# Moving the preparation of the output projection's right operands into the retention

## The reference

```python
for layer in range(DEPTH):                      # DEPTH = 2, x is (1024, 1024) float32
    h = rms_norm(x, norm_g[layer])
    z = h @ w_in[layer]
    ...                                         # attention -> oa, ya
    qr, kr, vr = ...                            # 4 retention heads of 128
    orr = bidirectional_retention(qr, kr, vr, lg_f, lg_b)
    orr = head_group_norm(orr, ret_gn_w[layer])
    yb = (jax.nn.silu(gr) * orr) @ w_branch_ret[layer]
    gates = jax.nn.sigmoid(gm).reshape(b, s, N_BRANCHES, d)
    merged = gates[:, :, 0] * ya + gates[:, :, 1] * yb
    x = x + merged @ w_out[layer]
return rms_norm(x, final_norm_g)
```

## Time and profile before

| what | value |
|---|---|
| median of 3 runs | 1856.19 us (1851.78 to 1858.89) |
| the profiled execution | 1854.67 us |
| its span in the profile | 1852.8 us |
| mean granted TensorE clock | 0.989 |
| PE busy | 1755.4 us (95%) |
| PE weight loads busy | 1555.3 us (84%) |
| DVE busy | 1262.6 us (68%) |
| ACT busy | 800.3 us (43%) |
| POOL busy | 671.9 us (36%) |
| moved by DMA | 113.08 MB, mean 61 GB/s |

### The profile page before, as it was taken

The page is one execution under the profiler, slowest core; times in us unless marked ns, Lnnn a source line. Parts: engine busy times, 40 slices in busy tenths (PEclk is TensorE's granted clock), DMA queues, the critical chain, the costliest instruction groups (busy, mean ns, idle before and its releaser), DMA issues.

```text
span 1852.8 us, 30202 instructions
## 1 busy us (share of the span) xinstructions
PE 1755.4 (95%) x10592; PEld 1555.3 (84%) x10592; DVE 1262.6 (68%) x2626; ACT 800.3 (43%) x1791; POOL 671.9 (36%) x581
## 2 busy tenths in 40 slices
PE   6799999999999999999989998999999999999986
PEld 5688978899999888887787888889999998888865
DVE  7878578725544387769986877795345544867798
ACT  4378448722122243333344873684222123433333
POOL 0048217724233323223601771484224322232240
PEclk9999999999999999999999999999999999999998
DMA  7000000011011323224130001001011023222322
GB/s 269 23 13 12 27 23 24 24 47 47 23 34 35 131 66 100 80 90 160 46 118 24 24 1 50 12 12 47 24 46 45 23 92 114 67 82 86 131 80 91
DMA packets 136666, 113.08 MB, mean 61 GB/s; under 512 B 16481, under 2 KB 115041, under 8 KB 136545
## 3 DMA queue, kind: packets, MB, share of 16 engines
q1 hardware_dynamic: 134144, 106.20, 17.9%
q10 hardware_dynamic: 2400, 5.31, 0.8%
HBM read 90.52 MB, written 20.97 MB: 60 GB/s over the span
## 4 chain that ended last, share of the span: by engine, by line
PE 71%; DVE 17%; issue 4%; POOL 3%; ACT 3%; DMA 2%; POOLq 0%; SPq 0%; DVEq 0%; ACTq 0%
PE ps L758 17%; PE ps L760 17%; PE ps L759 16%; PE ps L894 4%; PE ps L883 4%; PE ps L907 2%; DVE xh L2163 2%; PE ps L909 2%; PE ps L1000 2%; POOL pp L612 1%; PE ps L984 1%; DVE hT_lo L2150 1%; DVE us L1895 1%; DVE pT_lo L1807 1%; DVE lsum L2141 1%
## 5 line engine op out<-in xcount | busy, mean ns | idle before, releaser
L758 PE MATMUL ps<-w_hi,hT_hi 128*128 128x256 f32 (+1 forms) x1280 | 390.9, 305 | 13.8 <-DVE hT_lo L1666 4.8
L760 PE MATMUL ps<-w_hi,hT_lo 128*128 128x256 f32 (+1 forms) x1280 | 376.6, 294 | 0.0
L759 PE MATMUL ps<-w_lo,hT_hi 128*128 128x256 f32 (+1 forms) x1280 | 376.3, 294 | 0.0
L758 PEld LDWEIGHTS ps<-w_hi,hT_hi 128*128 128x128 f32 x1280 | 244.8, 191 | 19.0 <-DVE hT_lo L1666 7.0
L759 PEld LDWEIGHTS ps<-w_lo,hT_hi 128*128 128x128 f32 x1280 | 245.1, 191 | 0.3
L760 PEld LDWEIGHTS ps<-w_hi,hT_lo 128*128 128x128 f32 x1280 | 244.5, 191 | 0.0
L612 POOL TENSOR_SCALAR pp<-pp,rrc 128x1024 f32<-128x1024 f32 x128 | 144.1, 1126 | 164.5 <-DVE rrc L1812 157.3
L1807 DVE TENSOR_TENSOR pT_lo<-ps,pT_hi 128x512 fp32r<-128x512 f32 x256 | 164.1, 682 | 26.5 <-ACT pT_hi L1307 25.2
L558 POOL TENSOR_SCALAR w_hi<-raw 128x1024 fp32r<-128x1024 f32 x65 | 69.2, 1064 | 290.5 <-PE ps L760 254.6
L1799 DVE TENSOR_REDUCE nmx<-ps 128x1 f32<-128x1024 f32 x128 | 154.0, 1203 | 2.6 <-PE ps L883 2.6
L894 PE MATMUL ps<-idf,pp 128*128 128x128 f32 x1024 | 140.6, 278 | 15.5 <-DVE pT_lo L1807 9.0
(11 more groups left out here) (215 smaller groups left out, 4103.5 us busy)
## 6 DMA issues: line engine op xcount, KB each, us to landing
raw<-w_in SPq DMA_DIRECT2D x167, 256.0 KB, 3.3
xs<-xh SPq DMA_DIRECT2D x2, 4096.0 KB, 16.9
ys<-y_st SPq DMA_DIRECT2D x32, 256.0 KB, 2.1
hb<-ys SPq DMA_DIRECT2D x16, 512.0 KB, 4.6
xh<-xs SPq DMA_DIRECT2D x8, 1024.0 KB, 7.0
raw<-w_a SPq DMA_DIRECT2D x16, 256.0 KB, 3.2
raw<-w_r SPq DMA_DIRECT2D x16, 256.0 KB, 3.3
w<-w_o SPq DMA_DIRECT2D x4, 1024.0 KB, 6.2
```

The source lines that it names most:

```text
L758: nc.tensor.matmul(outp, ah, bh, start=(start and i == 0), stop=False)
L759: nc.tensor.matmul(outp, ah, bl, start=False, stop=False)
L760: last = nc.tensor.matmul(outp, al, bh, start=False, stop=(stop and i == len(pairs) - 1))
```

## The change

The right operands are no longer made in the output projection. During the retention they are made one row piece at a time and written to a tensor `wos` in the chip's memory, and in the output projection they are loaded from there, as they are, into the places that PE reads.

There are 28 items per layer: 4 row pieces k of w_out (K_R = 4, piece k belongs to head k) times 7 products in the order R_ORDER. One item is 128 rows x 512 columns of high and of low part. For each item: POOL makes the sum where it has one (`right_sum`, items 2 to 6 of a piece), ACT the high part (`right_hi`), DVE the low part (`right_lo`), and ACT issues the write to memory (`right_put`, 512 KB). ACT also loads piece k of w_out (`right_load`, 1 MB). Two staging places alternate, so item n waits until item n - 2 has been written (`r_free`). R_FIRST, R_SECOND and R_NEXT say at which tile each item stands: all seven of piece 0 in head 0's first pass at tiles 2 to 8, items 0, 1, 2 of piece h + 1 in head h's second pass at tiles 3, 5, 7, and items 3, 4, 5, 6 of piece h in head h's first pass at tiles 1, 3, 5, 6. The hardware loops of POOL, ACT and DVE over the heads are written out. The two `keep_out` steps wait for the items and their writes of that head.

```diff
+K_R = 4
+R_ORDER = (1, 5, 0, 2, 3, 4, 6)
+N_R = K_R * N_P
+R_FIRST = {2: 0, 3: 1, 4: 2, 5: 3, 6: 4, 7: 5, 8: 6}
+R_SECOND = {3: 0, 5: 1, 7: 2}
+R_NEXT = {1: 3, 3: 4, 5: 5, 6: 6}
...
+        def r_free(eng, L, n):
+            if L * N_R + n >= 2:
+                eng.wait_ge(r_out[n % 2], 16 * ((L * N_R + n) // 2))
...
 @@ sync: output projection
+                def right_in(p, halves=(0, 1)):
+                    for h in halves:
+                        c = right_wide(p, h)
+                        for s, to in enumerate(right_slot(p, h)):
+                            src = wos[p, :, s, 1024 * h:1024 * h + 1024].rearrange("p (b c) -> p b c", c=c)
+                            sp.dma_start(to.bitcast(F32), src).then_inc(o_r[R_SLOT[p]][h], 16)
...
+                    if m == 2:
                         sp.wait_ge(e_lo, (L + 1) * 2 * N_S)
+                        for b in range(2):
+                            sp.wait_ge(r_out[b], 16 * (L + 1) * (N_R // 2))
+                        right_in(0, (0,))
...
+                sp.wait_ge(g_p, x7 + 3)
+                right_in(0, (1,))
                 x_block(0, 1)
                 sp.wait_ge(g_p, x7 + 4)
                 x_block(1, 1)
+                sp.wait_ge(g_p, x7 + 7)
+                right_in(1)
                 x_block(0, 0)
+                right_in(2)
                 sp.wait_ge(d_mg, (L + 1) * N_G)
                 x_block(1, 0)
+                for p in range(3, N_P):
+                    if p != 4:
+                        sp.wait_ge(o_done, L * (4 * N_P) + 4 * N_P + 4 * ({3: 0, 5: 1, 6: 2}[p] + 1))
+                    right_in(p)
...
 @@ gpsimd
+                def right_sum(k, i):
+                    n = k * N_P + i
+                    blocks = RIGHT[R_ORDER[i]]
+                    if len(blocks) == 1:
+                        return
+                    pool.wait_ge(r_in, 16 * (L * K_R + k + 1))
+                    r_free(pool, L, n)
+                    (r, c, q) = blocks
+                    a, b = (wo_raw[:, 2 * x[0] + x[1]] for x in (r, c))
+                    nc.gpsimd.tensor_tensor(r_total(n), a, b, ALU.add if q > 0 else ALU.subtract).then_inc(r_sum, 1)
...
                             else:
                                 fill_lo(i % 2, i, n0 + U_C + fills * N_C + N_C + i)
+                        at = R_FIRST if h == 0 else R_NEXT
+                        if t in at:
+                            right_sum(h, at[t])
...
-                with pool.Fori(0, RH - 1) as h:
+                for h in range(RH - 1):
                     fill_qk(h)
+                    for i in R_SECOND.values():
+                        right_sum(h + 1, i)
                     rotate(h + 1, h)
...
 @@ scalar
+                def right_hi(k, i):
+                    n = k * N_P + i
+                    if len(RIGHT[R_ORDER[i]]) == 1:
+                        act.wait_ge(r_in, 16 * (L * K_R + k + 1))
+                        r_free(act, L, n)
+                    else:
+                        act.wait_ge(r_sum, (L * K_R + k) * 5 + i - 1)
+                    nc.scalar.copy(r_rows(n)[0], r_src(n)).then_inc(r_hi, 1)
+                def right_put(k, i):
+                    n = k * N_P + i
+                    act.wait_ge(r_hi, L * N_R + n + 1)
+                    act.wait_ge(r_lo, L * N_R + n + 1)
+                    a = 2 * (n % 2)
+                    act.dma_start(wos[R_ORDER[i], :, :, 512 * k:512 * k + 512], quad(ur_lo, 4)[:, a:a + 2].bitcast(F32)).then_inc(r_out[n % 2], 16)
+                def right_steps(at, t, k):
+                    if t - 1 in at:
+                        right_put(k, at[t - 1])
+                    if t in at:
+                        right_hi(k, at[t])
...
+                        right_steps(R_FIRST if done is None else R_NEXT, t, h)
...
 @@ vector
+                def right_lo(k, i):
+                    n = k * N_P + i
+                    dve.wait_ge(r_hi, L * N_R + n + 1)
+                    hi, lo = r_rows(n)
+                    V.tensor_tensor(lo, r_src(n), hi.bitcast(F32), ALU.subtract).then_inc(r_lo, 1)
+
                 def keep_out(h, half):
+                    for b in range(2):
+                        dve.wait_ge(r_out[b], 16 * ((L * N_R + min(h + 2, K_R) * N_P + 1 - b) // 2))
...
+                        at = R_FIRST if done is None else R_NEXT
+                        if t in at:
+                            right_lo(h, at[t])
...
+                        if h + 1 < RH and t in R_SECOND:
+                            right_lo(h + 1, R_SECOND[t])
```

More of the change, by code:

```diff
@@ L168, in build @@
             pT_lo = sb(p2, "pT_lo", [2, T, 256], F32R)
+        with ExitStack() as pz:
+            sb(pz, "below_wo", [2 * SEQ])
+            wo_raw = sb(pz, "wo_raw", [4, 512])
         ur_hi = sb(ctx, "ur_hi", [KA, SEQ], F32R)
@@ L205, in build @@
             w12 = sb(pg, "w12", [4, 512])
+        with ExitStack() as pg:
+            first_r = sb(pg, "first_r", [4, 512], F32R)
         gB = sb(ctx, "gB", [DM])
@@ L249, in build @@
             "g_sum", "g_hi", "g_wd", "g_wp", "g_p", "g_a", "g_d", "g_t"))
[L250 to L253, removed]
+        o_r = [[sem("o_r%d%d" % (i, h)) for h in range(2)] for i in range(4)]
+        r_in, r_sum, r_hi, r_lo = map(sem, ("r_in", "r_sum", "r_hi", "r_lo"))
+        r_out = [sem("r_out0"), sem("r_out1")]
+        o_sum, o_ahi, o_alo, o_done, o_post = map(sem, ("o_sum", "o_ahi", "o_alo", "o_done", "o_post"))
         f_y = sem("f_y")
@@ L1142, in last_product @@
                     pe.wait_ge(o_alo, L * (2 * N_P) + 2 * ORDER_A.index(p) + 2)
-                    pe.wait_ge(o_blo, L * (2 * N_P) + 2 * N_P + 2 * p + 2)
+                    for h in range(2):
+                        pe.wait_ge(o_r[R_SLOT[p]][h], 32 * (L * R_USES[R_SLOT[p]] + R_NTH[p] + 1))
                     for i in range(4):
@@ L1373, in update, with right_load @@
                     nc.scalar.copy(oc[:, t], ps[:, 4, 0:RD]).then_inc(c_oc, 1)
+                def right_load(k):
+                    if k:
+                        act.wait_ge(r_lo, L * N_R + k * N_P)
+                    src = w_o[bass.ds(L * DM, DM), :].rearrange("(q k p) (b c) -> p q k b c", p=P, k=K_R, c=512)
+                    act.dma_start(wo_raw[:].rearrange("p (q b) c -> p q b c", b=2), src[:, :, k]).then_inc(r_in, 16)
+                def right_hi(k, i):
[17 more added lines that the diff above has]
+                        right_hi(k, at[t])
                 def keep_out(h, half):
+                    act.wait_ge(r_lo, L * N_R + min(h + 2, K_R) * N_P)
                     act.wait_ge(consts_in, NCONST)
@@ L1400, in second_pass @@
                             update(h, t - 1)
+                        if h + 1 < RH:
+                            if h == 0 and t == 0:
+                                right_put(0, R_FIRST[T])
+                            if t == 0:
+                                right_load(h + 1)
+                            right_steps(R_SECOND, t, h + 1)
+                    if h + 1 < RH:
+                        right_steps(R_SECOND, T, h + 1)
+                right_load(0)
                 first_pass(0, None)
-                with act.Fori(0, RH - 1) as h:
+                for h in range(RH - 1):
                     second_pass(h)
@@ L1974, in _ @@
                 first_pass(0, None)
-                with dve.Fori(0, RH - 1) as h:
+                for h in range(RH - 1):
                     second_pass(h)
```

142 lines of the change are left out of this document (37 added, 105 removed).

## The result

The changed kernel takes **1952.2 us** (median of 5 runs, 1951.9 to 1958.0) where the kernel before takes 1856.2 (5 runs beside them, 1851.8 to 1858.9). The ratio is 1.052 with an interval of 1.050 to 1.054: slower by 5%. The forecast was 1948 us with a range of 1908 to 1983. The profiled execution of after took 1951.9 us with a span of 1949.9, against a span of 1852.8 before, so its span is 97.1 us longer.

The account below looks back on a forecast made before the run. PE was taken to bound the retention, but not alone the output projection, where DVE is busy without a pause. 1854.7 - 18 (output projection) + 96 (retention steps) + 16 (clock) = 1948.7, stated as 1948 us, range 1908 to 1983.

Parts of the forecast that it names:

- The output projection: Making operands there goes away: 18 us gained of PE's 19.4 us lost over two layers, bounds 12 and 20.
- The loads put at nothing: Output projection's operand loads, 14 MB per layer, were to arrive in time and cost 0 us.
- rival D: Output projection: loads come late and products wait as before, retention slow too; 1966 us, chance 0.06.
- The walk through head 2's first pass: Retention, event by event on before's clock: scores of tile 1 come 12.5 us late.
- The gap at `cross`: Retention, head 2's first pass: PE stands 2.7 us waiting for DVE's delayed cross products.
- the contention that the prediction weighed for the subtractions only: Retention: DVE's two-SBUF-input subtractions slowed beside POOL, 15 us per layer at most.
- The passes: Retention first passes: head 0 loses 13 us, heads 1 to 3 12.5 each; 101 in two layers, taken as 96.
- the bookkeeping: Retention queue-by-queue count of delays: 50.5 us per layer, 101 in two; feared to overstate a pass by 1.5 us.
- The clock: Retention: PE's clock drops around its gaps, costing 16 us in all, bounds 0 and 25.
- 14 gaps: Retention: 7 clock-lowering PE gaps per layer, two per first pass of heads 1 to 3, one in head 0; up to 24 us.
- B: Rival: the added steps hide in the retention, leaving only the output projection's 18 us gain; 1837 us, chance 0.07.
- C: Rival: partial cover, retention costs 20 us and just pays back the 18 us gain; 1857 us, chance 0.03.

Follow-up runs that it names:

- lagged kernel: Changed kernel with keeping waiting only for its rows, and sum, cast, subtraction and write a tile or two apart in first passes of heads 1 to 3: 1895.4 us.
- steps in other places: Changed kernel with piece 0's stages lagged in head 0's first pass, pieces 1 to 3 in second passes, five staging pairs, keeping waiting for its own rows: 1829.4 us.
- the kernel with the sum ahead of the fill: Changed kernel with POOL's sum of a step placed before the weight fill of the same tile instead of behind it: 1943.5 us.
- the two kernels with products in the wait: Changed kernel with 20, then 14, identity products per head on PE ahead of its wait for tile 0's decayed scores: 1953.7 and 1946.9 us.

## Why the prediction was right, and where it was off

**The bound and the place.** PE sets the time in the retention and DVE's in-order queue holds it: shown by the lagged kernel and by the one with the steps in other places, which do the same work for +4.9 to +7.5 and 0.0 us a pass.

**The output projection** was forecast at -18, with 10.4 + 9.0 lost by PE as the most that could go. All 19.4 went. The loads put at nothing cost nothing; rival D is out, with PE at 66.0 of 66.0 us from 905 to 971 and DMA up to 1.09. That was nearer than the working has it: side by side the loads of 512 KB took 4.6 to 14.9 us each, where it had 5.1 for 1 MB alone, and product 1 had 2.7 us to spare. What I had not counted is 3.6 us in the tail and 2.3 between the layers. Before, DVE ran behind PE with its additions: in the last layer it finished the last of them at 1837.6, 2.2 us after PE's last product. In after it is PE that DVE waits for:

```profile
1936.23 0.69 DVE L2218 SCALAR_TENSOR_TENSOR xh<-ps,xh 128x512 f32<-128x512 f32 x1 [1.82 <-PE ps L1177]
```

**The walk through head 2's first pass**, on before's clock (after less 30.24 us, the difference at the rotation of tile 1):

| event | before | forecast | measured |
|---|---|---|---|
| `cross` starts | 488.21 | 493.7 | 493.41 |
| rotation of tile 4 | 499.86 | 507.25 | 506.47 |
| rotation of tile 5 | 503.72 | 511.1 | 510.18 |
| rotation of tile 6 | 506.63 | 515.55 | 514.68 |
| rotation of tile 7 | 510.33 | 521.4 | 521.69 |
| `keep_out` | 511.78 | 524.85 | 525.86 |
| scores of tile 1 | 513.33 | 525.9 | 526.86 |

The gap at `cross` was forecast at 2.7 us and is 2.34. Two errors nearly cancel: a sum takes 1.29 us where I took 1.42 from a row of another tile form, and `normed` takes 2.52 us for four instructions beside POOL's sum where it took 1.53 before, twice in a pass. The second is the contention that the prediction weighed for the subtractions only and then left out. The walk also has no wait of PE for ACT's copy of the transposes, which is 1.99 us here and comes just before the 5.05: PE would otherwise have stood the longer for the decayed scores, so it changes nothing of the sum.

**The passes.** Heads 1 to 3 were put at 12.5 us each plus the clock, head 0 at 13. Measured with the clock: 16.1, 15.3, 15.5 and 16.2. The sum of steps and clock was 101 + 16 = 117 by the bookkeeping, and I took 96 + 16 = 112 as I feared to have overstated a pass. I had understated it, by 0.8 us a pass: measured are 124.5, of which 17 are the clock (below), so 107.5 for the steps where the bookkeeping had 101. For head 0 one link was wrong: I let the chain start with the landing of the load. Its first cast stood behind ACT's copy of tile 0's transposes (start 380.98, which is 383.1 on before's clock, 0.2 us after the landing I had assumed). One turn took 4.13 us (subtractions at 387.90, 392.03 and 396.15) instead of 4.5. The last two subtractions then took 1.62 and 2.58 us beside POOL's last sum and a fill.

**The clock** was put at 16 us from 14 gaps. The scores-to-scores distance behind the wait for the decayed scores is 1.5 to 2.3 us too long in each of the 8 passes, 6.7 us in layer 0 and 7.9 in layer 1. Behind the gap at `cross` the clock fell in two passes of six. From the last scores of one head to the first of the next are 38.7 us in the other four and 39.6 and 40.3 in these two, 2.4 us more. Head 0's projections ahead of the wait ran at the half clock as well (granted 0.50), but PE stood 3.57 us behind them, which hid it. So it is 6.7 + 7.9 + 2.4 = 17 us. Size and mechanism hold, the count of gaps doesn't: ten of the 14 cost something. That their sum comes so near is partly luck.

**The rivals.** B (the steps hide) decided at 1.3 to 2.7 us of delay at tile 1; the delay was 5.2. But B's time, 1837, is what the better placed steps reach and pass, since its price left out the 5.9 us of tail and hand-over between the layers and 1.4 of the output projection. C is out: it had 20 us for the retention, which costs six times that.

The total: forecast 1854.7 - 18 + 96 + 16 = 1948.7; measured -19.4 for the output projection, +124.5 for the retention, -5.9 between layers and in the tail, -2.1 at the start. The retention term was 12.5 us short, 1 of it the clock. The output projection gave 1.4 more than its term, and the gains I had not listed took back 8, of which 2.1 are the scatter of the start. That the total comes within 4 us of the measured one is in good part luck; the mechanism isn't.

## What to carry to other kernels

A step that is moved off a busy stage is not priced by its busy time but by what stands behind it in each in-order queue that it enters. Work of 2.7 us in a pass cost 15.6 us next to its producer, 4.9 with each stage a tile or two behind the one before, and 0.0 in a pass where the engine had idle time at that very point. Before such a move, follow one pass on every engine's timeline, and look for the tile at which the engine sits idle and not for the pass in which its share is low.

## What the runs showed of the hardware

A subtraction of 128x512 with both inputs in SBUF takes 0.69 us on DVE alone. Started 0.73 us into a 2.40 us subtraction on POOL it took 2.22, ending 0.55 us after POOL's, which was not delayed. The end lay as far behind POOL's in three more cases: 0.54 and 0.56 us in head 0 of after (1.62 us beside a sum, 2.58 beside a fill), 0.55 in the kernel with the steps in other places (1.78 us, started 0.06 us into a sum of 1.29). Turning the order of two instructions on POOL so moved most of the cost from a wait to a duration.

In the lagged kernel PE's clock went from full to half over a wait of 1.51 us at the decayed scores, after 1.48 us of work in the 2 us ahead of it. A gap of the same 1.51 us at `cross`, in the kernel with the sum ahead of the fill, left it full in all six first passes, and one of 2.34 us in after, behind 2 us in which PE didn't pause, in four of six. With 28 matmuls in the wait for the decayed scores the clock was full behind it in three of four heads. The Trainium skill has the fall and the rise of the clock follow PE's activity (TensorE: Matmul & The Clock Gate, What's actually happening); the two kernels with products in the wait agree. The heavy load of DMA (1.05, 381 GB/s) did not slow a matmul: those of L1156 took 389 ns at the least, in the middle and at the most.
